# A two-layer encoder trunk: 46 of its product tiles come out channel-major, with weights stationary

## What is computed

```
for l in range(2):
    if l % 2 == 0:
        u = x @ ev_w_in        # 2048 x 6144: conv a, conv gate, q, f, i, g
        a_out = silu(layer_norm(causal_depthwise_conv31(a * sigmoid(gate))))
        f = lb + (1 - lb) * sigmoid(f_logit); k = 1 - f; q = silu(q)
        b_out = hgrn2(q, k, log f, i) gated by g      # 8 heads of 128, in chunks
        mix = concat(a_out, b_out) @ ev_w_out
    else:
        u = x @ od_w_in        # 2 x (q, k, v) of 8 heads of 128, and 8 forget logits
        mix = concat(forgetting_attention, chunked_attention) @ od_w_out
    x = layer_norm(ALPHA * x + mix)
    x = layer_norm(ALPHA * x + square(relu(x @ mlp_w1)) @ mlp_w2)
```

## Time and profile before

| | us |
|---|---|
| median of 3 runs | 2288.47 (2286.49 to 2291.45) |
| the profiled execution: its time | 2288.11 |
| the profiled execution: its span, first to last instruction | 2286.4 |
| mean granted TensorE clock | 0.994 |

### The profile page before, as it was taken

The page is one execution under the profiler, slowest core; times in us unless marked ns, Lnnn a source line. Parts: engine busy times, 40 slices in busy tenths (PEclk is TensorE's granted clock), DMA queues, the critical chain, the costliest instruction groups (busy, mean ns, idle before and its releaser), DMA issues.

```text
span 2286.4 us, 28509 instructions
## 1 busy us (share of the span) xinstructions
PE 2249.9 (98%) x10331; PEld 1864.2 (82%) x10331; DVE 1341.9 (59%) x1472; ACT 1057.0 (46%) x1146; POOL 36.6 (2%) x68
## 2 busy tenths in 40 slices
PE   8999999999999999999999999999999999999997
PEld 7888788788888888888878888887888888888886
DVE  4898986854445544445565445568454454544455
ACT  4555565454344444344434444444534444543541
POOL 2000000000000001000000000000000000000000
PEclk9999999999999999999999999999999999999999
DMA  7555545565556656655546555565555565555553
GB/s 242 166 158 158 172 133 177 164 209 190 196 184 221 194 190 199 207 185 184 186 127 193 166 177 165 164 227 156 190 190 195 184 221 195 183 193 200 184 184 110
DMA packets 213040, 418.50 MB, mean 183 GB/s; under 512 B 12793, under 2 KB 13361, under 8 KB 211904
## 3 DMA queue, kind: packets, MB, share of 16 engines
q1 hardware_dynamic: 211120, 406.90, 55.8%
q0 software_dynamic: 1808, 10.04, 1.3%
HBM read 414.79 MB, written 2.10 MB: 182 GB/s over the span
## 4 chain that ended last, share of the span: by engine, by line
PE 91%; DVE 4%; DMA 2%; ACT 1%; issue 1%; DVEq 0%; SPq 0%; ACTq 0%
PE gemm L1326 29%; PE gemm L1328 29%; PE gemm L1327 29%; PE pair L1712 1%; DVE w_lo L802 1%; DVE lnp L1067 1%; DMA raw<-in_mlp_w 1%; PE pair L1481 1%; ACT w_hi L493 1%; PE pair L1398 1%; PE pair L1438 0%; PE pair L1554 0%; PE pair L1626 0%; PE pair L1599 0%; DVE X L864 0%
## 5 line engine op out<-in xcount | busy, mean ns | idle before, releaser
L1199 DVE TENSOR_TENSOR w_lo<-raw,w_hi 128x1024 fp32r<-128x1024 f32 x488 | 596.7, 1225 | 484.7 <-ACT w_hi L716 453.6
L716 ACT ACTIVATE w_hi<-raw 128x1024 fp32r<-128x1024 f32 x492 | 522.1, 1061 | 631.4 <-PE gemm L1328 608.7
L1326 PE MATMUL gemm<-w_hi,x_hi 128*128 128x512 f32 x1792 | 710.4, 396 | 7.0 <-DVE w_lo L802 6.5
L1328 PE MATMUL gemm<-w_hi,x_lo 128*128 128x512 f32 x1792 | 701.1, 391 | 0.0
L1327 PE MATMUL gemm<-w_lo,x_hi 128*128 128x512 f32 x1792 | 700.3, 391 | 0.0
L1326 PE MATMUL gemm<-w_hi,c_hi 128*128 128x512 f32 x1280 | 502.0, 392 | 4.6 <-DVE X L830 3.4
L1328 PE MATMUL gemm<-w_hi,c_lo 128*128 128x512 f32 x1280 | 499.6, 390 | 0.0
L1327 PE MATMUL gemm<-w_lo,c_hi 128*128 128x512 f32 x1280 | 499.5, 390 | 0.0
L802 DVE TENSOR_TENSOR w_lo<-raw,w_hi 128x1024 fp32r<-128x1024 f32 x280 | 340.3, 1223 | 199.3 <-ACT w_hi L493 193.5
L493 ACT ACTIVATE w_hi<-raw 128x1024 fp32r<-128x1024 f32 x276 | 289.3, 1056 | 305.8 <-PE gemm L1328 268.9
L1326 PEld LDWEIGHTS gemm<-w_hi,x_hi 128*128 128x128 f32 x1792 | 338.0, 189 | 82.3 <-issue 6.1
(11 more groups left out here) (194 smaller groups left out, 784.3 us busy)
## 6 DMA issues: line engine op xcount, KB each, us to landing
raw<-in_mlp_w SPq DMA_DIRECT2D x512, 512.0 KB, 4.7
raw<-in_ev_w_in SPq DMA_DIRECT2D x96, 512.0 KB, 3.8
raw<-in_od_w_in SPq DMA_DIRECT2D x96, 512.0 KB, 4.1
raw<-in_ev_w_out SPq DMA_DIRECT2D x32, 512.0 KB, 4.1
raw<-in_od_w_out SPq DMA_DIRECT2D x32, 512.0 KB, 3.7
lnp<-in_ln_mix_g POOLq DMA_DIRECT2D x2, 1024.0 KB, 6.4
lnp<-in_ln_mix_b POOLq DMA_DIRECT2D x2, 1024.0 KB, 6.3
lnp<-in_ln_mlp_g POOLq DMA_DIRECT2D x2, 1024.0 KB, 7.9
```

The lines of the kernel that those rows point to most:

```text
L716: act.activation(hi_of_chunk(s), raw[:, s % RING], ACT.Copy).then_inc(hi_ready, 1)
L1199: dve.tensor_tensor(lo_of_chunk(s), raw[:, s % RING], hi_of_chunk(s).bitcast(F32), ALU.subtract).then_inc(lo_ready, 1)
L1326: pe.matmul(acc[:, r, :], hi[:, k + c, rows], high, start=begin, stop=False)
L1328: return pe.matmul(acc[:, r, :], lo[:, k + c, rows], high, start=False, stop=end)
```

## The change

46 tiles are computed by a new `turned_chunk`: a 128-column piece of the weights is the stationary operand and the 256 tokens stream, so the tile comes out with channels on the partitions (`turned` is the same PSUM seen as 4 x 256). A chunk takes 24 matmuls of 256 columns, a tile 192. These are tiles 0 to 5, 8 and 9 of the even layer, q and k of all groups of the odd layer, and all tiles of the MLPs' first product but the first of each MLP, which still comes out by rows and is transposed once (`first_hidden`, now behind the fourth chunk of the second tile). The transposes of the other tiles and the copies ahead of them are gone. The odd layer's groups are now in the order v, q, k, and their attention steps sit four slots later. The scan of the even layer sits two slots earlier.

```
-ODD_TILES = [base + third * KDIM for base in (0, N, FOX_F + HEADS, FOX_F + HEADS + N) for third in range(3)]
+ODD_TILES = [base + third * KDIM for base in (0, N, FOX_F + HEADS, FOX_F + HEADS + N) for third in (2, 0, 1)]
+TURNED = [{0, 1, 2, 3, 4, 5, 8, 9}, {i for i in range(12) if i % 3}]
...
+            def turned_chunk(acc, act_, k, s, first, last):
+
+                hi, lo = act_
+                for c in range(CK):
+                    begin, end = first and c == 0, last and c == CK - 1
+                    for m in range(4):
+                        cols = slice(m * P, (m + 1) * P)
+                        high, low = hi_of_chunk(s)[:, c, cols], lo_of_chunk(s)[:, c, cols]
+                        pe.matmul(acc[:, m, :], high, hi[:, k + c, :], start=begin and m % 2 == 0, stop=False,
+                                  skip_group_check=True)
+                        pe.matmul(acc[:, m, :], high, lo[:, k + c, :], start=False, stop=False, skip_group_check=True)
+                        ins = pe.matmul(acc[:, m, :], low, hi[:, k + c, :], start=False, stop=end and m % 2 == 1,
+                                        skip_group_check=True)
+                ins.then_inc(chunk_used, 1)
...
-                act.wait_ge(h_ready_row, half + 1)
-                evac(0, i, urow[0], ACT.Copy, row_ready)
-                upto(s0 + 13)
-
                 if half == 1:
                     act.wait_ge(z_ready, 8)
-                act.wait_ge(pair_full[0], USE[0][f"F{half}"] + 1)
-                act.activation(Dm, pair[0][:, :], ACT.Sigmoid).then_inc(sig_ready, 1)
-                upto(s0 + 14)
+                evac(0, i, Dm.rearrange("p (r n) -> p r n", r=RT), ACT.Sigmoid, sig_ready)
+                upto(s0 + 12)
...
-                if s == 79:
+                if s == 77:
                     forget(1, FORGET_SLOT[1])
...
-                dve.tensor_tensor(urow[1], gemm[(TILE0[0] + i) % 2][:, :, :], urow[0], ALU.mult
-                                  ).then_inc(h_ready_row, 1)
+                dve.tensor_tensor(hpad[half][:, :, CONV_W - 1:], turned[(TILE0[0] + i) % 2], h_turned[0], ALU.mult
+                                  ).then_inc(pad_ready, 1)
...
-                if 1 <= i <= NT:
-                    act.wait_ge(pair_full[0], b * NT + (USE[0]["h", layer, 0] + i))
-                    act.activation(c_hi[:, 4 * (i - 1):4 * i, :], quad[0], ACT.Copy).then_inc(h_hi, 1)
+                if by_rows and i == 1:
+                    hi_of(0, ("h", layer), c_hi[:, 0:4, :], h_hi)
...
+                        if not (by_rows and i < 2):
+                            act.wait_ge(h_ready, b * NT + (layer * FB * NT + i - 1))
                         act.activation(urow[i % 2], gemm[t % 2][:, :, :], ACT.Relu).then_inc(relu_done, 1)
                         act.wait_ge(relu_done, b * NT + (layer * FB * NT + i + 1))
                         act.activation(urow[i % 2], urow[i % 2], ACT.Square).then_inc(h_row, 1)
+                        if not (by_rows and i == 0):
+                            act.wait_ge(h_row, b * NT + (layer * FB * NT + i + 1))
+                            act.activation(c_hi[:, 4 * i:4 * i + 4, :], h_turned[i % 2], ACT.Copy).then_inc(h_hi, 1)
...
-                    if r == 9:
-                        rows_to(0, ("q", g), urow[0], 6 + 3 * g + 1)
-                        if g == 1:
-                            forget_columns(1)
-                    if r == 17:
-                        rows_to(0, ("k", g), urow[1], 6 + 3 * g + 2)
-                    if r == 20:
+                    if r == 9 and g == 1:
+                        forget_columns(1)
+                    if r == 24:
                         scores(g)
-                    if r == 25:
+                    if r == 29:
                         probs(g)
-                    if r == 27:
+                    if r == 31:
                         attend(g)
...
+                    if i < NT:
+                        for c in range(CPT):
+                            s = base + i * CPT + c
+                            pe.wait_ge(lo_ready, b * (2 * NT * CPT) + (s + 1))
+                            turned_chunk(turned[t % 2], X_, CK * c, s, c == 0, c == CPT - 1)
+                            if first_block and i == 1 and c == RING - 1:
+                                first_hidden()
+                        return
```

More of the change, by code:

```diff
@@ L130, in pieces @@
     return [("x", which, i) for i in range(p, NO if which else NP, 2)]
[L133 to L137, removed]
+USE = [numbered(*pieces(0, 0), "O0", "mean", "variance", "O1",
+                *pieces(1, 0), ("h", 0), *pieces(2, 0),
+                *[(name, g) for g in range(4) for name in ("scores", "probs", "out")],
+                *pieces(3, 0), ("h", 1)),
        numbered(*pieces(0, 1), "params", *[("level", half, k) for half in range(2) for k in range(10)],
@@ L180, in trunk @@
         both = used[0]
+        h_turned = [u.rearrange("p r n -> p (r n)").rearrange("p (m t) -> p m t", m=4) for u in urow]
         L = cut(HG * S)
@@ L242, in trunk @@
         quad = [p[:, :].rearrange("p (k t) -> p k t", k=4) for p in pair]
+        turned = [g[:, :, :].rearrange("p r n -> p (r n)").rearrange("p (m t) -> p m t", m=4) for g in gemm]
         raw_full = [sem(f"raw_full{i}") for i in range(RING)]
@@ L578, in query @@
                 upto(s0 + 11)
[L580 to L584, removed]
+                evac(0, i, qT.rearrange("p h t -> p (h t)").rearrange("p (r n) -> p r n", r=RT), ACT.Silu, q_ready)
             def exps(half, k):
@@ L744, in _ @@
                 upto(s0 + 11)
-                evac(1, 3 * g, urow[0], ACT.Copy, row_ready)
+                evac(1, 3 * g, vrow, ACT.Copy, row_ready)
                 if g == 0:
@@ L821, in add_row @@
                 if r == 0:
-                    dve.wait_ge(rows_done, t + 1)
+                    dve.wait_ge(rows_done, NT * ((PARTS + FB) * layer + part) + j + 1)
                 else:
@@ L1177, in add_last, with mlp_tile @@
                 tile_stats(j, r)
-            def mlp_tile(layer, b, i, last=False, split_before=0):
+            def mlp_tile(layer, b, i, by_rows=False, last=False, split_before=0):
                 base = SLOT_MLP[layer]
@@ L1183, in mlp_tile @@
                     dve.wait_ge(h_hi, b * NT + (layer * NT * FB + i))
-                    dve.tensor_tensor(c_lo[:, 4 * (i - 1):4 * i, :], quad[0],
+                    dve.tensor_tensor(c_lo[:, 4 * (i - 1):4 * i, :], quad[0] if by_rows and i == 1 else h_turned[(i - 1) % 2],
                                       c_hi[:, 4 * (i - 1):4 * i, :].bitcast(F32), ALU.subtract
@@ L1335, in chunk_rows @@
                     ins = products(acc, act_[0], act_[1], r, k, s, c, first and c == 0, last and c == CK - 1)
-                if last and r == 0:
+                if last and r == 0 and act_ is C_:
                     ins.then_inc(rows_done, 1)
@@ L1363, in _ @@
             for layer in range(DEPTH):
-                for name in HIDDEN[layer]:
-                    read_out[0][name] = (h_ready, FB * NT * layer + name[2] + 1)
+                read_out[0]["h", layer] = (h_ready, FB * NT * layer + 1)
             for g in range(4):
-                read_out[0].update({("q", g): (qk_ready, 2 * g + 1), ("k", g): (qk_ready, 2 * g + 2),
-                                    ("scores", g): (scores_read, 2 * g + 1), ("probs", g): (pT_act, g + 1),
+                read_out[0].update({("scores", g): (scores_read, 2 * g + 1), ("probs", g): (pT_act, g + 1),
                                     ("out", g): (cat_ready, 4 + g)})
@@ L1384, in acquire @@
                     pe.wait_ge(x_sum, (PARTS + FB) * NT - 1 + i)
-                return gemm[(TILE0[layer] + i) % 2]
+                return (turned if i in TURNED[layer] else gemm)[(TILE0[layer] + i) % 2]
             def pair_free(p, name):
@@ L1668, in _ @@
                                 first_tile(c)
-                            chunk(acc, X_, CK * c, s + c, c == 0, c == CPT - 1)
+                            if i in TURNED[layer]:
+                                pe.wait_ge(lo_ready, s + c + 1)
+                                turned_chunk(acc, X_, CK * c, s + c, c == 0, c == CPT - 1)
+                            else:
+                                chunk(acc, X_, CK * c, s + c, c == 0, c == CPT - 1)
                             behind(s + c - s0)
@@ L1741, in mlp_tile @@
                                 final = layer == 0 and last_block and i == 2 * NT - 1 and r == RT - 1 and c == CPT - 1
-                                chunk_rows(acc, operand, r, CK * c, s, c == 0, c == CPT - 1,
+                                chunk_rows(acc, C_, r, CK * c, s, c == 0, c == CPT - 1,
                                            halfway=(lambda: row_piece(2, 0)) if final else None)
-                            if half == 0 and r == 0 and 1 <= i <= NT:
-                                hidden(b, i, first_block)
                 for i in range(2 * NT):
```

111 lines of the change are left out of this document (37 added, 74 removed).

## The result

| | before | after |
|---|---|---|
| median, us | 2288.47 | 2300.0 (2299.66 to 2301.78) |
| the profiled execution: its time | 2288.11 | 2301.78 |
| its span | 2286.4 | 2300.0 |
| mean granted TensorE clock | 0.994 | 0.995 |

The changed kernel takes 1.0054 times as long as the kernel before, with an interval of 1.004 to 1.0067. The forecast was 2281.6 us. The time lies inside the range, but on the other side of zero, 3.7 us from rival (a). The profiled execution of after is the slowest of its five, so its span grew by 13.6 us where the median grew by 11.5.

The account below looks back on a forecast made before the run. The prediction took TensorE, busy 98% of the span, as the bound: matmul starts times their distance, plus a few stalls. MLPs -6.2, odd layer -0.8 and even layer +0.5 made -6.5 us, from 2288.11 to 2281.6; range 2268 to 2304.

Parts of the forecast that it names:

- rival (a): Turned stretches: the weight load decides, 120 ns per matmul, adding 58.7 instead of 36.7 us, 2303.7 us; chance 0.27.
- Part 1: 46 tiles in 256-column matmuls at 117.5 ns, a pair 235.0 instead of 226.7 ns: +36.7 us.
- Part 5: Mixers: turned tiles' costs less saved transposes, odd layer -0.8 us, even layer +0.5 us.
- Rival (b): Cost goes with columns alone: 113.3 ns per 256-column matmul, Part 1 is 0, about 2245 us; chance 0.08.
- Part 2: Transposes that go, 0.90 us a block of 8: -27.0 us in the MLPs, -12.6 in the mixers.
- Part 3: First transposes of each MLP, now later in the tile, no longer wait for ScalarE: -3.1 us.
- Part 4: MLPs: the reordered and later ACT and DVE work stays hidden from PE; cost nothing.
- Part 5, odd layer: The scores' copy is ready 0.5 us before its slot, no wait added; 6.4 - 7.2 = -0.8 us.
- Part 5, even layer: DVE hides PE's costs and savings in slots 24 to 39 and 64 to 79; outside +0.5 us; scan stall stays.
- rival (c): Even layer's scan collision changes: 2275.8 us if the stall goes, 2287.4 if a second opens; chance 0.10, half each way.
- theory F: Expectation tested in `widths`: a matmul costs a fixed 13.3 ns plus its columns at 2.4 GHz.

Follow-up runs that it names:

- widths: Changed kernel with ten tiles of the MLPs' first products in other widths and forms, and `forget_logits` with one weight address; one execution took 2371.95 us.
- run 2: Same run as `rows_late`: kernel before with only the first transposes of each MLP moved behind the second half's chunks; 2283.78 us, ratio 0.9986.
- rows_late: Kernel before with only the first transposes of each MLP moved behind the second half's chunks; 2283.78 us, ratio 0.9986.
- joint_rows: Kernel before with mixers by rows, the MLPs in the form of `joint` and the first block late; 2278.67 us, ratio 0.996 against before.
- mixers_turned: Changed kernel with both MLPs by rows again and the late first block; 2287.61 us, ratio 1.0007 against before.
- joint: Changed kernel; in the MLPs' 30 turned tiles `w_hi` is loaded once for `x_hi` and `x_lo` in one 512-column matmul; 2283.73 us, ratio 0.9989 against before.
- rows_odd: `rows_late` with `x_hi`, `x_lo`, `c_hi` and `c_lo` moved by 8 columns (32 bytes); 2323.82 us, ratio 1.0152 against before.
- runs 5 and 6: Run 5: changed kernel with `w_hi` and `w_lo` moved by 32 bytes, 2322.58 us, ratio 1.0147; run 6: `rows_odd`, 2323.82 us, ratio 1.0152.

## Why the prediction was wrong

**Part 1 failed, by its size.** "I take 117.5, the mean over the form that is nearest": the form was nearest in shape and format, but not in its addresses. The distance is 120.0 ns, the bound that I had put down to rounding. With it, 4416 pairs cost 58.7 us instead of 36.7. Part 5 hides four of the 46 tiles, so 42 pay the difference in the sum: 42 x 96 x 5.0 ns = 20.2, and -6.5 + 20.2 = +13.7 us, for a span that grew by 13.6. That it fits so closely is partly luck, since the terms do not fit one by one: +8.8 in the MLPs where the sum has +8.2, +3.6 in the odd layer for +3.0, +1.6 in the even one for +2.4 (5.1 for the four tiles that Part 5 does not hide, less 2.7 for the blocks). I had the clue in hand: 226.7 is 213.3 + 13.3, and 13.3 again on 106.7 is 120.0. Read so, the row of the 512-column matmul said 120.0, `forget_logits` said 117.5, and the two had to be weighed; I used the first only as a ratio (bound 113.3) and so never saw the fixed price.

**Rival (a)** named 120 ns and 2303.7 us, with the right consequence. Its 22.1 us count all 46 tiles, against Part 5, and are 1.9 too many. Its mechanism, the load decides, is not what the widths show: there is a floor, at 110 to 111 ns, but 256 columns lie above it and pay the same 13.3 ns as 512. **Rival (b)**, cost by columns alone, is out.

On the Trainium skill, "TensorE: Matmul & The Clock Gate", section "Wait — 56ns, not 53.3ns?": its 2.5 ns per warm matmul do not agree with these runs in fp32r with a load each, which show 13.3 ns at both widths. The load time of that page's section "LDWEIGHTS (loading the stationary operand)", some 107 ns, lies near the floor of 110 to 111 ns in `widths`; no trace here shows the time of a load alone. The prediction read this as speaking against the change, and the direction was right, but the 120.0 ns are above that floor.

**Part 2** held: 21.76 + 0.90 = 22.66 us for a tile by rows with its transposes, against 23.04 turned. Each turned MLP tile loses 0.38 us, 30 of them 11.4 us.

**Part 3** held, alone (run 2) and in the profile after, where PE goes from the last product of the fourth chunk into the transposes and has no idle time before them, against 1.62 us in the earlier trace rows:

```profile
475.79 0.28 PE L1339 MATMUL gemm<-x_hi,w_lo 128*128 128x256 f32 x1
475.91 1.04 PE L1690 MATMUL pair<-ident,scr 128*128 128x128 f32 x8
476.70 0.36 PE L1336 MATMUL gemm<-x_hi,w_hi 128*128 128x256 f32 x1
```

**Part 4** held but for one thing. No new wait for ACT or DVE came into the MLPs. With 120.0 ns the sum there is 2880 x 13.3 = 38.3, less 27.0 and 3.1, or +8.2, and the windows show +8.8. Some 0.3 to 0.5 of the rest is a single gap in the second MLP, where its loop jumps back:

```profile
1929.42 0.39 PE L1314 MATMUL gemm<-w_hi,c_lo 128*128 128x512 f32 x1
1930.13 0.38 PE L1336 MATMUL gemm<-x_hi,w_hi 128*128 128x256 f32 x1 [0.33 <-issue]
```

No such gap stands at the jump in the first MLP, nor in either MLP before, so the jump alone does not explain it, and what does was not tried.

**Part 5, odd layer**, held in its mechanism: no wait for the scores appears. 768 pairs x 13.3 = 10.2, less 7.2, is +3.0, and the window shows +3.6.

**Part 5, even layer**, was wrong in where VectorE hides PE's work, though its sum came near. It put slots 24 to 39 (tiles 3 and 4) and 64 to 79 (tiles 8 and 9) behind VectorE, since that is busy 94% and 98% there. Tiles 3 and 4, PE only, before and after:

```profile
81.48:127.36 45.88, 45.80 (x210) 1.00 0.56 165
...
83.64:129.72 46.08, 46.08 (x387) 1.00 0.52 162
```

46.08 us are 384 x 120.0 ns: PE pays every one of them and waits for nobody, with VectorE busy 43.1 us beside it. Tiles 8 and 9 take 46.9 us instead of 45.7, also without idle time. A busy engine hides nothing where no one waits for it. What came back is elsewhere: tile 5 takes 30.7 us in both kernels though it is turned (1.2 us), and PE's idle time in it falls from 0.8 to 0.25 us; in tiles 4 and 9 of before, short waits for `w_lo` and the slow starts behind them are gone (1.0); tiles 10 and 11 take 56.2 us instead of 57.9, 0.9 of it the block of transposes (0.7 more); the first tile has the rest (0.5). Over the 12 input tiles that is 309.1 us instead of 307.7, or +1.4, where costs paid in full would be 8 x 1.28 - 5.4 = +4.8. Other executions agree: 307.9 and 307.5 by rows (`rows_late`, `joint_rows`), 309.0 and 309.2 turned (`mixers_turned`, `joint`).

The stall came back near slot 80 as said, but smaller. DVE in after, around the second scan, beside the earlier trace rows:

```profile
255.68 2.29 DVE L968 TENSOR_TENSOR_SCAN scr<-rstm,scr 128x1024 f32<-128x1024 bf16 x1
257.88 4.82 DVE L1055 SCALAR_TENSOR_TENSOR lnp<-scr,lnp 128x256 f32<-128x256 f32 x12
262.61 1.22 DVE L790 TENSOR_TENSOR w_lo<-raw,w_hi 128x1024 fp32r<-128x1024 f32 x1
```

and PE behind it, beside the earlier trace rows:

```profile
263.98 0.47 PE L1312 MATMUL gemm<-w_hi,x_hi 128*128 128x512 f32 x1 [1.85 <-DVE w_lo L790]
264.29 0.40 PE L1313 MATMUL gemm<-w_lo,x_hi 128*128 128x512 f32 x1
```

PE is idle 1.85 us instead of 3.37, and starts again 0.31 us apart instead of 0.60. In exchange two waits open in tile 11, where before had none:

```profile
296.13 0.50 PE L1312 MATMUL gemm<-w_hi,x_hi 128*128 128x512 f32 x1 [0.36 <-DVE w_lo L790]
...
299.68 0.41 PE L1475 MATMUL pair<-scr 128*128 128x64 f32 x2 [0.53 <-DVE scr L996]
```

With them PE is idle 2.9 us in tiles 10 and 11, 3.4 before, so the first half of rival (c) came true in part, and something like its second half at another place. The lowered clock comes only at 265.0 and lasts 3.4 us in the records, against 6.8 before. It cost nothing here: in `mixers_turned`, with the same instructions and the same 1.86 us idle, the clock is not lowered there at all, and tiles 10 and 11 take the same 56.2 us. Rival (c) had priced it at 2.4.

**The range** held the time because both ends of Part 1 were carried through it. The chances did not use them well: one 5.6 us stretch over another buffer was given the weight of a measurement of the turned tile.

## What to carry to other kernels

Count matmuls, not columns: in fp32r with a load for each, two of 256 columns cost 13.3 ns more than one of 512 (240.0 against 226.7), and below 256 columns a start saves at most 10 ns more, since 110 to 111 ns is the floor. A block of eight 128 x 128 transposes at 0.90 us is cheaper than avoiding it by splitting 96 matmuls, at 1.28 us. Where two products share a stationary operand, stream both through one load. Count a cost as hidden only where the trace shows the engine waiting, not where another is busy. And take a price from a form whose buffers lie alike, or carry both prices to the end.

## What the runs showed that I had not expected

- Addresses are part of the cost. The same 128 x 256 form takes 120.0 or 117.7 ns by where its weight pieces start (runs after and `widths`), and 32 bytes on the stationary operand turned 226.7 into 231.4 ns for 512 columns (`rows_odd`, where the padding can have moved other buffers too); runs 5 and 6 lost 1.5% of the time each.
- A stream has paces that it keeps. In `joint_rows` the same instructions run at 353 ns a pair in one block of tiles and at 346 in another. 20 of its 30 joint tiles ran at the worse one, and two more up to their middle; at the better one, 22.19 us a tile instead of 22.62, they would take about 9 us less by this estimate. How to hold it is open.
- A stream of 448 columns beside 64 took 203 to 207 ns where the line of theory F has 200.0; 384 (175 for 173.3) and 320 (146 for 146.7) lie close to it. No tile of 448 columns alone was run, so whether the mixing costs this is open.
